# A hybrid decoder step on one core: VectorE's mixer steps in another order, S5 states and outputs in later slots, and MoE tokens gathered for two experts at once

## What is computed

```python
def _mixer(h, ...):
    ua, va, xb, gb, uc, gl = split(h @ w_in)          # 5 x 512 columns and 3 x 1024 gates
    va = _layernorm(gelu(va), ...)
    ya = gelu(ua) * _chunk_spatial_gate(va, a_ws, a_bs)      # "mixed"
    xc = causal_dwconv(xb)                                    # "conv"
    hs = _rg_lru(xc)                                          # gates r, i and a scan: "lru"
    yb = hs * gelu(gb)
    ys = _s5(uc, ...)                                         # 32 groups, 64 complex states each
    z = gelu(ys)
    yc = z * sigmoid(z @ c_glu_w + c_glu_b)                   # "glu"
    p = einsum('ntkc,kcd->ntkd', stack([ya, yb, yc]), w_branch)
    g = sigmoid(gl + b_gate)
    return sum(g * p over the 3 branches) @ w_out             # "wo"

x = x + _mixer(rmsnorm(x))
x = x + swiglu(rmsnorm(x))        # layer 0: dense, 2816 wide
x = x + moe(rmsnorm(x))           # layer 1: top 2 of 8 experts, each SwiGLU 1408 wide
```

## Time and profile before

| | us |
|---|---|
| median of three timed runs | 1450.63 |
| lowest and highest of them | 1450.41 and 1464.84 |
| the profiled execution, as timed | 1451.03 |
| its span in the profile | 1449.3 |
| first projection to slot 5, layer 0 and layer 1 | 126.61 and 96.19 |
| slot 5 to the end of y_of(2), layer 0 and layer 1 | 85.69 and 88.12 |
| from there to the first chunk of wo, layer 0 and layer 1 | 102.34 and 101.94 |
| one expert of the MoE | 57.54 |

### The profile page before, as it was taken

The page is one execution under the profiler, slowest core; times in us unless marked ns, Lnnn a source line. Parts: engine busy times, 40 slices in busy tenths (PEclk is TensorE's granted clock), DMA queues, the critical chain, the costliest instruction groups (busy, mean ns, idle before and its releaser), DMA issues.

```text
span 1449.3 us, 23175 instructions
## 1 busy us (share of the span) xinstructions
PE 1320.0 (91%) x9162; PEld 1284.4 (89%) x9162; DVE 985.8 (68%) x1302; ACT 690.0 (48%) x787; POOL 63.9 (4%) x117
## 2 busy tenths in 40 slices
PE   4785789999999999898869999999999999999995
PEld 4774789999999999797769989999999999999994
DVE  6799943466655555489872445648888888788873
ACT  4254122344443243345522334557667667666561
POOL 2000500100000000000210200000000000000000
PEclk9897799999999999999989999969999999999998
DMA  6320573545655346132474534538788787787850
GB/s 215 106 88 30 122 171 107 130 153 173 202 162 166 121 155 205 58 106 88 104 121 141 144 114 147 218 125 319 284 308 316 264 336 292 286 319 282 309 224 38
DMA packets 47456, 262.64 MB, mean 181 GB/s; under 512 B 6048, under 2 KB 6624, under 8 KB 34832
## 3 DMA queue, kind: packets, MB, share of 16 engines
q1 hardware_dynamic: 42048, 243.55, 48.6%
q0 software_dynamic: 4752, 15.37, 5.9%
q10 hardware_dynamic: 576, 2.62, 0.4%
HBM read 255.89 MB, written 5.62 MB: 180 GB/s over the span
## 4 chain that ended last, share of the span: by engine, by line
PE 77%; DVE 15%; DMA 3%; ACT 2%; issue 2%; DVEq 0%; SPq 0%; ACTq 0%
PE bank L1836 22%; PE bank L1838 22%; PE bank L1837 22%; DMA raw<-w_in_in 3%; DVE w_lo L1083 2%; PE s_bank L2081 2%; PE bank L2081 1%; PE bank L1848 1%; PE bank L1827 1%; ACT w_hi L766 1%; PE bank L1954 1%; PE s_bank L1954 1%; DVE cross L1320 1%; PE s_bank L2117 0%; PE bank L1949 0%
## 5 line engine op out<-in xcount | busy, mean ns | idle before, releaser
L1089 DVE TENSOR_TENSOR mw_lo<-mraw,mw_hi 128x2816 fp32r<-128x2816 f32 x96 | 295.8, 3088 | 61.3 <-ACT mw_hi L773 60.3
L1836 PE MATMUL bank<-hn_hi,w_hi 128*128 128x320 f32 x656 | 220.3, 336 | 54.9 <-DVE w_lo L1083 42.1
L773 ACT ACTIVATE mw_hi<-mraw 128x2816 fp32r<-128x2816 f32 x96 | 245.0, 2552 | 16.1 <-PE bank L1838 16.0
L1083 DVE TENSOR_TENSOR w_lo<-raw,w_hi 128x1024 fp32r<-128x1024 f32 x128 | 154.4, 1223 | 93.4 <-ACT w_hi L766 90.3
L1837 PE MATMUL bank<-hn_lo,w_hi 128*128 128x320 f32 x656 | 214.3, 327 | 0.0
L1838 PE MATMUL bank<-hn_hi,w_lo 128*128 128x320 f32 x656 | 213.7, 326 | 0.0
L1836 PEld LDWEIGHTS bank<-hn_hi,w_hi 128*128 128x128 f32 x656 | 133.8, 204 | 62.7 <-DVE w_lo L1083 46.7
L1836 PE MATMUL bank<-mw_hi,x_hi 128*128 128x352 f32 x512 | 168.7, 330 | 1.9 <-DVE x_lo L1700 1.9
L1838 PE MATMUL bank<-mw_hi,x_lo 128*128 128x352 f32 x512 | 165.8, 324 | 0.0
L766 ACT ACTIVATE w_hi<-raw 128x1024 fp32r<-128x1024 f32 x128 | 132.8, 1052 | 69.3 <-PE bank L1838 47.7
L1837 PE MATMUL bank<-mw_lo,x_hi 128*128 128x352 f32 x512 | 165.2, 323 | 0.0
(11 more groups left out here) (443 smaller groups left out, 2820.1 us busy)
## 6 DMA issues: line engine op xcount, KB each, us to landing
mraw<-w_moe_in SPq DMA_DIRECT2D x96, 1408.0 KB, 7.2
raw<-w_in_in SPq DMA_DIRECT2D x88, 512.0 KB, 4.3
uraw<-w_gu_in SPq DMA_DIRECT2D x44, 512.0 KB, 3.5
raw<-w_br_in SPq DMA_DIRECT2D x24, 512.0 KB, 3.9
...
```

The source lines that it names most:

```text
L773: act.activation(mw_hi[c % MSPLIT][:, :], mraw[slot][:, :], ACT.Copy).then_inc(hi_ready, 1)
L1083: dve.tensor_tensor(w_lo[g % SPLIT][:, :], raw[slot][:, :], w_hi[g % SPLIT][:, :].bitcast(F32), ALU.subtract).then_inc(lo_ready, 1)
L1089: dve.tensor_tensor(mw_lo[c % MSPLIT][:, :], mraw[c % MRAW][:, :], mw_hi[c % MSPLIT][:, :].bitcast(F32), ALU.subtract).then_inc(lo_ready, 1)
L1836: pe.matmul(out, w_h[k], x_h[k], start=start and k == 0, stop=False)
```

## The change

**Slots and order in the mixer.** The constants say where PE's extras stand:

```diff
-ST_TRANS, ST_K, ST_U, ST_INJECT, ST_T, ST_Y, ST_Z, ST_GLU = 1, 3, 5, 7, 9, 12, 17, 20
+ST_TRANS, ST_K, ST_INJECT, ST_Y, ST_GLU = 2, 12, (14, 16), 18, 23
```

On DVE `output_powers(0)` leaves its place behind the statistics of va for slot 8, `output_powers(1)` goes from slot 1 to 9, `input_powers(1)` from ahead of slot 0 into it, `conv` from 0 to 1, `normalised` into slot 2 with w_lo's between its rows, `ahead` into slot 10, the turns of layer 0 from slot 2 to 11; `glu` stands behind slot 23 and the low halves of yc in the first step of branch 2, behind its `split`:

```diff
@@ -1537,27 +1557,34 @@
                         y_low(ug, ya_hi[:, :, :], ya_lo[:, :, :], 1)
                     if s > 8 and s % 2 and s < SLOT_N - 1:
                         split(l, upto((s - 8) // 8, s % 8) + 1)
-                    if s == 1:
-                        output_powers(1, (16, 16))
...
+                    if s == 0:
+                        input_powers(1, (15, 15))
+                    if s == 2:
+                        normalised(lambda b: split(l, 16 + b // 2))
+                    if s == 8:
+                        output_powers(0, (upto(0, 1), upto(0, 1)))
+                    if s == 9:
+                        output_powers(1, (upto(0, 2), upto(0, 2)))
+                    if s == 10:
+                        ahead()
+                    if s == 11 and l == 0:
+                        turns(lambda w: split(l, upto(0, {0: 4, 2: 4, 4: 4, 8: 5, 16: 5}[w])))
                         router_low()
                     if s == ST_K:
                         k_diag()
-                    if s in (ST_INJECT, ST_INJECT + 1):
-                        states(s - ST_INJECT)
-                    if s == ST_GLU + 1:
-                        glu()
-                    if s == ST_GLU + 3:
-                        for m in range(KB):
-                            y_low(yc[:, m], yc_hi[:, m], yc_lo[:, m], 3 + m)
-                    if s == 0:
+                    if s in ST_INJECT:
+                        states(ST_INJECT.index(s))
+                    if s == 1:
                         dve.wait_ge(a_free, A.of[("xb", l, 3)][1] + 1)
                         conv()
                     if s == 5:
                         lru()
+                glu()
                 for m in range(KD):
                     split(l, upto(2, m))
+                    if m == 0:
+                        for k in range(KB):
+                            y_low(yc[:, k], yc_hi[:, k], yc_lo[:, k], 3 + k)
```

The turns have fewer operations: the double angle in three instead of five, and the table from powers without squarings, in widths of 1, 2, 4, 8 and 15:

```diff
                 for _ in range(3):
-                    chain(dve.tensor_tensor(t, cs, cs, ALU.mult))
-                    chain(dve.tensor_tensor(t2, sn, sn, ALU.mult))
-                    chain(dve.tensor_tensor(t3, cs, sn, ALU.mult))
-                    chain(dve.tensor_tensor(cs, t, t2, ALU.subtract))
-                    chain(dve.tensor_tensor(sn, t3, t3, ALU.add))
+                    chain(dve.scalar_tensor_tensor(t, sn, -2.0, sn, ALU.mult, ALU.mult))
+                    chain(dve.scalar_tensor_tensor(sn, cs, 2.0, sn, ALU.mult, ALU.mult))
+                    chain(dve.tensor_scalar(cs, t, 1.0, None, ALU.add))
+                between(0)
...
-                w = 2
+                w = 1
                 while w < NP:
 
-                    cr, ci = er[:, :, w // 2], ei[:, :, w // 2]
-                    chain(dve.tensor_tensor(t, cr, cr, ALU.mult))
-                    chain(dve.tensor_tensor(t2, ci, ci, ALU.mult))
-                    chain(dve.tensor_tensor(t, t, t2, ALU.subtract))
-                    chain(dve.tensor_tensor(t2, cr, ci, ALU.mult))
-                    chain(dve.tensor_tensor(t2, t2, t2, ALU.add))
-                    full = [P, DEPTH * NST, w]
-                    pr, pi = (v.unsqueeze(2).to_broadcast(full) for v in (t, t2))
-                    lo, hi = slice(0, w), slice(w, 2 * w)
-                    tt = zr[:, :, :, :].rearrange("p c s n -> p (c s n)")[:, 0:DEPTH * NST * w]
-                    tt = tt.rearrange("p (n w) -> p n w", w=w)
+                    v = min(w, NP - 1 - w)
+                    if v <= 0:
+                        break
+                    lo, hi = slice(1, v + 1), slice(w + 1, w + 1 + v)
+                    full = [P, DEPTH * NST, v]
+                    pr, pi = (e[:, :, w:w + 1].to_broadcast(full) for e in (er, ei))
+                    tt = cross[:, :, :].rearrange("p s n -> p (s n)")[:, 0:DEPTH * NST * v].rearrange("p (n w) -> p n w", w=v)
                     chain(dve.tensor_tensor(er[:, :, hi], er[:, :, lo], pr, ALU.mult))
                     chain(dve.tensor_tensor(tt, ei[:, :, lo], pi, ALU.mult))
                     chain(dve.tensor_tensor(er[:, :, hi], er[:, :, hi], tt, ALU.subtract))
                     chain(dve.tensor_tensor(ei[:, :, hi], er[:, :, lo], pi, ALU.mult))
                     chain(dve.tensor_tensor(tt, ei[:, :, lo], pr, ALU.mult))
                     chain(dve.tensor_tensor(ei[:, :, hi], ei[:, :, hi], tt, ALU.add))
+                    if w > 1:
+                        between(w)
                     w *= 2
-                    between(w)
```

ACT's copies of yc go behind the slots (L929 to 932), and ACT waits for v_ready in slot 4. On POOL the write of k_scratch with its wait for k_ready goes from the head of a layer's queue to behind the ends of the convolution, and z is written in two halves:

```diff
                 pool.sem_inc(ends_read, 1)
+                pool.wait_ge(k_ready, l + 1)
+                if l == 0:
+                    pool.wait_ge(k_cleared, 16 * DEPTH)
+                pool.dma_start(k_dram[l, :, :, :, (LC - 1) * HG:].rearrange("g h k n -> (g h) k n"),
+                              kp[:, :, :, :].rearrange("p k j h -> p k (j h)")).then_inc(k_written, 16)
                 pool.wait_ge(k_written, 16 * (l + 1))
                 pool.wait_ge(states_full, 2 * (l + 1))
...
-                pool.wait_ge(z_ready, KB * (l + 1))
                 for i in range(4):
+                    pool.wait_ge(z_ready, KB * l + 2 * (i // 2) + 2)
                     pool.dma_start(z_dram[l, i % 2, :, :, 2 * (i // 2):2 * (i // 2) + 2].rearrange("t h k j c -> (t h) (k j c)"),
                                   zy[:, i]).then_inc(z_written, 16)
```

```diff
-            def gather(no, out, h):
+            def gather(no, out, q):
...
-                for j in range(4):
-                    c = slice(P * (4 * h + j), P * (4 * h + j) + P)
+                for j in range(2):
+                    c = slice(P * (2 * q + j), P * (2 * q + j) + P)
                     for i, t in enumerate((tok_hi, tok_lo)):
                         for b in range(3):
-                            mm = pe.matmul(out[:, SLOTS * j:SLOTS * j + SLOTS], t[:, b, c], disp[:, b],
+                            mm = pe.matmul(out[:, 2 * SLOTS * j:2 * SLOTS * j + 2 * SLOTS], t[:, b, c],
+                                           disp[:, b].rearrange("p e n -> p (e n)"),
                                            start=i == 0 and b == 0, stop=i == 1 and b == 2)
...
-                    if not last:
-                        pe.wait_ge(disp_ready, it + 2)
-                        gather(*small_no(r, u, "G0"), 0)
+                    if e and not last:
+                        pe.wait_ge(disp_ready, p + (2 + N_PAIRS * r))
+                        gather(*small_no(r, p, e, "G0"), 0)
                     transposed(3)
                     down(0)
                     down(1)
                     scatter(0)
+                    if e and not last:
+                        gather(*small_no(r, p, e, "G1"), 1)
                     down(2)
                     scatter(1)
-                    if not last:
-                        gather(*small_no(r, u, "G1"), 1)
+                    if e and not last:
+                        gather(*small_no(r, p, e, "G2"), 2)
+                        gather(*small_no(r, p, e, "G3"), 3)
                     down(3)
```

More of the change, by code:

```diff
@@ L310, in build @@
         lnr = sb("lnr", [P, 3])
+        s5_last_at = at[0]
         s5_last = sb("s5_last", [P, 2, NST, NLAST])
@@ L412, in build @@
         assert cur <= th_at
+        x_lo = [sb(f"x_lo{q}", [P, 2, 2, SLOTS], F32R, where)
+                for q, where in enumerate((cur, cur + 16 * SLOTS, sp_at, zr_at))]
+        assert cur + 32 * SLOTS <= s5_last_at
         bank = [ctx.enter_context(nc.psum_tensor(f"bank{i}", [P, 512], F32)) for i in range(5)]
@@ L559, in items @@
         def items(engine, r, item):
-            with engine.Fori(0, NEXP - 1) as u:
-                item(u, u if isinstance(r, int) and r == 0 else u + NEXP * r, False)
-            item(NEXP - 1, (NEXP - 1) + NEXP * r, True)
+            base = 0 if isinstance(r, int) else NEXP * r
+            with engine.Fori(0, N_PAIRS - 1) as p:
+                for e in range(2):
+                    item(p, e, 2 * p + e, 2 * p + (base + e), False)
+            for e in range(2):
+                u = NEXP - 2 + e
+                item(N_PAIRS - 1, e, u, base + u, e == 1)
         def rounds(engine, round_):
@@ L1044, in item @@
                             hidden_high(c // 2 - 2)
+                        if c == 11 and e and not last:
+                            tokens_high(*small_no(r, p, e, "G1"), 1)
                         if c > 8:
@@ L1781, in item @@
                             low(it + 1, c + 2 - N_CHUNK)
-                    if not last:
-                        tokens_low(*small_no(r, u, "G1"), r, 3 + 2 * u, 1)
+                    if e and not last:
+                        tokens_low(*small_no(r, p, e, "G2"), r, 6 + 4 * p, 2)
+                        tokens_low(*small_no(r, p, e, "G3"), r, 7 + 4 * p, 3)
                     result_low(3)
@@ L2089, in round_, with item @@
```

(7 more changed lines are left out.)

184 lines of the change are left out of this document (93 added, 91 removed).

## The result

The changed kernel takes 1521.8 us (median of 4 runs, 1517.99 to 1523.35) against 1452.34: the ratio on record is 1.0464, interval 1.0424 to 1.0503. The direction was forecast, the size was not: 1483 us was predicted, with 1501 us as the upper end. The profiled execution took 1523.0 us, its span is 1521.3. A profile is of one execution, and in some of the experiments that one lies 8 to 9 us off the median; it is said where it matters.

What follows compares the result with a forecast made beforehand. It took DVE's lateness ahead of slot 5 as what the mixer could win, and PE work as the experts' bound. 1451.0 + 9.6 + 23.7 - 1.5 = 1482.8, forecast 1483 us, own range 1466 to 1495, with rivals 1433 to 1501.

Steps and rivals of the forecast that it cites:

- Fronts: Mixer from first projection to slot 5: 87.3 and 84.5 us in layers 0 and 1, gains of 39.3 and 11.7.
- Idle time behind slot 5: PE's idle time in the mixer behind slot 5, all stall terms together: 55.8 us in layer 0, 44.6 in layer 1.
- slots 8 to 12: Mixer: DVE's load stays while PE loses the injects, so PE idles 16 us a layer.
- behind the turns: Slot 11 on: SP's queue waits for k_ready, delaying weight loads; 12 us in layer 0, 0.8 in layer 1.
- states: Slots 14 and 16: DVE's 8.7 us step between two w_lo's holds up PE, 9.3 us a layer.
- toep: y_of in slot 18 waits for the toep transfers issued behind inject(1), 6.5 us a layer.
- z: PE at glu waits for z's writes and reads on POOL, 6.9 us a layer.
- yc: Between glu and branch 2, DVE's glu(), ACT's copies, w_lo's and y_low hold PE up 5.1 us a layer.
- the mixer's sum: All mixer terms added: +9.6 us in layer 0, +23.7 in layer 1, with low clock cost taken as today's.
- slower still: the clock: Rival: more mixer stalls lower PE's clock, some seven times 2.3 us, giving 1499 us; chance 12%.
- The MoE: Gathers for expert pairs save PE work but lose cover for hid: -1.5 us together, ends -19 and +6.
- The faster rival: Late chains (k_ready, toep, z, yc) are hidden because DVE already delays PE: 1433 us; chance 25%.

Runs made afterwards that it cites:

- e10: The changed kernel with inject(1) and states(1) in slot 15 instead of 16: 1505.64 us (1.04).
- e11: As e9, with layer 0's inject(0) and states(0) in slot 13 instead of 14: 1449.01 us (0.9991).
- e4: The changed kernel with ACT's gelus of z(1) and z(3) right behind those of z(0) and z(2), a slot earlier: 1506.73 us (1.035).
- e3: The changed kernel with glu's two weight chunks merged later in SP's order, slot 18 instead of 14: 1514.08 us (1.0412).
- e6: The changed kernel with the next w_lo made in the middle of each states() on DVE: 1520.48 us (1.0441).
- e9: The changed kernel with e3, e4, w_lo's inside states() and lru(), slots by layer, earlier last splits, layer 1 partly reverted: 1441.26 us (0.9932).

## Why the prediction was right in direction and wrong in size

- **Fronts.** Predicted 87.3 and 84.5 us, measured 92.4 and 84.9. The three waits of layer 0 are as reckoned (3.28, 1.98 and 3.89 us, together 9.15 for 9.0). Its miss of 5 us is in the matmuls: 82.6 us at a clock of 0.92, where 78.3 at full clock were reckoned.
- **Idle time behind slot 5.** The sum had 55.8 and 44.6 us; measured 53.4 and 44.2. Term by term for layer 0: slots 8 to 12 16, measured 13.3 (5.64, 3.30, 4.33); behind the turns 12, measured 11.9; states 9.3, measured 8.3 (4.14, 4.15); toep 6.5, measured 7.4; z 6.9, measured 6.0; yc 5.1, measured 5.6. In layer 1 the same places measured 13.7, 2.1 (for 0.8), 8.3, 7.8, 6.8 and 5.6. The mechanisms of toep, z, k_ready, the states and yc were tried by e10 and e11, e4, e3, e6 and e9, and held; of the wait behind the turns a third is DVE and not the queue. The term of slots 8 to 12 was not tried by itself.
- **The step that failed** is one sentence of the mixer's sum: "What a low clock behind these stalls costs I take as today's." It is 19.6 and 17.5 us more than today's. That is 37 of the 40 us between 1483 and the profiled 1523; the front's 5 come on top, and the rest nets to -2. The whole miss is PE's busy time: by the sum it was to be 518.6 us in the two mixers (fronts of 78.3 at full clock, k_of 3.5 each, the rest as in the earlier trace rows), and it is 558.5.
- **The rival "slower still: the clock"** named this mechanism and put it at 16 us: four more stalls in layer 1 and two or three more in layer 0, at 2.3 us each from gate chunks. Both factors were low. The count: in the two mixers there are 19 waits of over 3 us where there were 10 (the one at the start of each layer left out), and behind slot 5 nine in layer 0 and eight in layer 1, where there were two in each. The price: a gate chunk of 24 matmuls behind a stall of 4 to 6 us costs 2 to 3 us more (6.34 and 6.16 us here for 3.5), as the earlier trace rows showed, but y_of(0) behind its stalls of 7.4 and 7.8 us ran at 0.50 throughout and cost 7.8 and 6.2 us more than before. The 23 us that are then left of the 37 would be some 2.1 for each of the 11 other stalls added; that is worked out from these numbers, and no run tried the gate chunks' part alone.
- **The MoE.** -1.5 predicted; the seven full experts take 407.2 us against 402.7, the start 3.3 less: +1.2. The waits were met (2.46 and 1.03 for hid, 1.8 for ym_lo); the first even expert ran at a clock of 0.94 and took 59.1 us where the second took 56.0 (the first takes 56.0 in e3, e4 and e9). The Trainium skill's figure for a stream of 128-column matmuls (TensorE: Matmul & The Clock Gate, back-to-back issue gap) would have made the saving an estimated 2 us instead of 4.8 a pair. The trace decides: in the rows below three matmuls of 256 columns take 0.36 us, 119 ns each, so a pair's 48 need 5.7 us against 10.5. The saving was there: 19 us by this count, of which 13.4 show in PE's busy time, since three of the even experts ran below full clock. PE's idle time in the seven experts, 21.9 us for 4.0, ate it.

```profile
1127.22 0.52 PE L2111 MATMUL bank<-disp,tok_hi 128*128 128x256 f32 x3
1127.58 0.52 PE L2111 MATMUL bank<-disp,tok_lo 128*128 128x256 f32 x3
```

- **Two slips** of the prediction that change little: its terms for the MoE add up to -1.9 and not -1.5, and from 735.78 to 758 are 22.2 us, not 22.7 (with the change toep landed 23.4 and 24.6 us after its issue began).
- **The faster rival**, that late chains are hidden by one another, was half true: in e6 and e11 stall time taken out ahead of toep came back as a wait for toep. It did not carry a gain.
